# Visiting sixteen experts round by round over their four groups, and scaling their input rows by column chunks during the output projection

## The reference, cut to what matters

```python
h = rmsnorm(x, norm2_g[l]) * (1 + scale2) + shift2
x = x + gate2 * hier_moe(h, ...)

def hier_moe(h, w_rg, b_rg, w_re, b_re, w_gate, w_up, w_down):
    t = h.reshape(bsz * L, D)
    g_prob = softmax(t @ w_rg + b_rg)
    g_top, g_idx = lax.top_k(g_prob, 1)                      # one of 4 groups
    e_in = (the 4 expert logits of that group)
    e_top, e_idx = lax.top_k(softmax(e_in), TOP_K_INNER)     # two of its 4 experts
    e_id = g_idx * EXPERTS_PER_GROUP + e_idx
    hid = silu(t @ w_gate[e]) * (t @ w_up[e]) * gate[e]
    out = sum over e of hid @ w_down[e]
```

## Time and profile before

| | |
|---|---|
| median of 3 executions | 1426.71 us (1423.45 to 1427.87) |
| time of the profiled execution | 1427.36 us |
| its span, first to last instruction | 1425.3 us |
| granted TensorE clock, mean | 0.928 of full |
| TensorE matmul busy | 1195.7 us (84%) |
| DVE / ACT / POOL busy | 311.0 / 201.0 / 115.9 us |
| bytes moved | 401.09 MB |

### The profile page before, as it was taken

One profiled execution on the slowest core, in us unless ns is written; L12 is line 12 of the kernel. 1 busy time (PEld: TensorE's weight loads), 2 busy tenths in 40 slices (PEclk: granted clock), 3 DMA queues, 4 the chain that ended last, 5 costly groups with the idle time before them and its releaser, 6 DMA issues.

```text
span 1425.3 us, 16027 instructions
## 1 busy us (share of the span) xinstructions
PE 1195.7 (84%) x6320; PEld 643.4 (45%) x6321; DVE 311.0 (22%) x623; ACT 201.0 (14%) x385; POOL 115.9 (8%) x129
## 2 busy tenths in 40 slices
PE   2688999999999999999992299999988787787740
PEld 0235666665545455545542244444544444444420
DVE  0101221131122224120018510111111211111128
ACT  2002111012021222100012100110111111111102
POOL 2010000000000002000005100000000000000016
PEclk9778999989999999999996599999999999999975
DMA  9988787747657529652530468877999999999953
GB/s 332 421 339 274 286 343 277 278 163 280 251 206 284 220 71 360 229 188 79 221 118 33 177 252 302 311 278 293 384 407 413 411 414 400 390 412 412 426 205 114
DMA packets 71717, 401.09 MB, mean 281 GB/s; under 512 B 6489, under 2 KB 6713, under 8 KB 39645
## 3 DMA queue, kind: packets, MB, share of 16 engines
q1 hardware_dynamic: 63216, 368.59, 66.1%
q0 software_dynamic: 6944, 23.99, 5.1%
q10 hardware_dynamic: 1520, 7.98, 1.5%
HBM read 394.85 MB, written 17.22 MB: 289 GB/s over the span
## 4 chain that ended last, share of the span: by engine, by line
PE 65%; DMA 26%; DVE 6%; issue 1%; ACT 1%; POOL 0%; SPq 0%; POOLq 0%; DVEq 0%
PE bank L815 20%; DMA arena<-in_w_up_dram 20%; PE bank L892 10%; PE bank L1163 8%; PE bank L819 5%; PE bank L810 5%; DMA arena<-in_w_ada_dram 5%; PE bank L1160 5%; PE bank L1186 4%; PE bank L836 1%; PE bank L1183 1%; PE bank L910 1%; DVE arena L1480 1%; DVE arena L1481 1%; PE bank L1146 1%
## 5 line engine op out<-in xcount | busy, mean ns | idle before, releaser
L815 PE MATMUL bank<-arena 128*128 128x512 f32 x640 | 287.1, 599 | 0.0
L1160 PE MATMUL bank<-arena 128*64 128x256 f32 x1536 | 185.5, 399 | 60.6 <-DMA arena<-in_w_gate_dram 33.2
L815 PEld LDWEIGHTS bank<-arena 128*128 128x128 f32 x640 | 118.7, 191 | 136.5 <-issue 135.2
L1160 PEld LDWEIGHTS bank<-arena 128*64 128x64 f32 x1536 | 112.5, 143 | 138.3 <-DMA arena<-in_w_gate_dram 44.3
L892 PE MATMUL bank<-arena 128*128 128x320 f32 x512 | 142.3, 437 | 3.8 <-DVE arena L1258 3.8
L810 PE MATMUL bank<-arena 128*32 128x512 f32 x768 | 103.0, 679 | 44.2 <-DMA arena<-in_w_ada_dram 32.2
L892 PEld LDWEIGHTS bank<-arena 128*128 128x128 f32 x512 | 97.3, 191 | 50.7 <-issue 7.2
L1163 PE MATMUL bank<-arena 128*128 128x512 f32 x256 | 113.0, 602 | 6.9 <-issue 6.9
L1183 PE MATMUL bank<-arena 128*64 128x512 f32 x384 | 85.0, 595 | 6.0 <-DVE arena L1629 6.0
L1626 DVE SCALAR_TENSOR_TENSOR arena<-bank,arena 128x512 f32<-128x512 f32 x16 | 12.0, 751 | 347.7 <-PE bank L1160 232.7
L1163 PEld LDWEIGHTS bank<-arena 128*128 128x128 f32 x256 | 49.3, 193 | 69.4 <-issue 69.4
(11 more groups left out here) (314 smaller groups left out, 855.4 us busy)
## 6 DMA issues: line engine op xcount, KB each, us to landing
arena<-in_w_ada_dram SPq DMA_DIRECT2D x48, 2048.0 KB, 14.7
arena<-in_w_gate_dram SPq DMA_DIRECT2D x32, 2048.0 KB, 26.3
arena<-in_w_up_dram SPq DMA_DIRECT2D x32, 2048.0 KB, 27.1
arena<-in_w_down_dram SPq DMA_DIRECT2D x32, 2048.0 KB, 26.1
arena<-in_w_in_dram SPq DMA_DIRECT2D x20, 2048.0 KB, 7.8
arena<-in_w_out_dram SPq DMA_DIRECT2D x8, 2048.0 KB, 8.9
arena<-mod_final POOLq DMA_DIRECT2D x6, 1024.0 KB, 11.7
arena<-expert_rows SPq DMA_DIRECT2D x8, 512.0 KB, 7.8
```

Source lines behind the costliest of these rows:

```text
L815: return mm(bank[:, :], lhsT=xT_[:, t, OFF[j]:OFF[j] + P], rhs=w, start=start, stop=stop)
L1160: last = mm(PB[bank][64 * h:64 * h + 64, 0:HALF], lhsT=XeT[:, t0 + t, 0:64], rhs=slots_w[slot][:, t, HALF * h:HALF * h + HALF], start=star ...
```

## The change

Experts are visited as 0, 4, 8, 12, then 1, 5, 9, 13, and so on: SP loads weights in that order, and `by_visit` writes the columns of `top1` and `top2` so that column `i` of every table belongs to visit `i`. The scale of `h2p` is applied by column chunks in natural column order (`scaled(q)`), three DVE instructions behind each chunk of the output projection; factor and shift follow in one instruction per tile (`shifted(j)`) inside the routing. Tile 2 leaves ACT and POOL, no tile lies in W1 any more, all three stores are issued by ACT, `Xe` moves to another place and is cleared earlier, the transposes read every 16th column, and TensorE reads the number of passes before its first transposes.

```diff
-        h2p = [at(SA, D), at(MX + 2048, D), at(SLOT, D)]
+        h2p = [at(SA, D), at(HT + 4096, D), at(HT + 6144, D)]
...
@@ SP
-                    if isinstance(i, int) and s == W1:
-                        sp.wait_ge(h2_stored[2], 16)
...
-            expert(0, 0)
-            with sp.Fori(1, NE) as e:
-                expert(e, e)
+            for g in range(4):
+                expert(4 * g, g)
+            with sp.Fori(1, 4) as a:
+                for g in range(4):
+                    expert(a + 4 * g, 4 * a + g)
@@ POOL
             pool.wait_ge(x1_ready, 12)
-            pool.wait_ge(ssq2, 12)
-            pool.memset(arena[:, SA + 2048:MX], 0.0).then_inc(cleared, 1)
...
-            pool.tensor_tensor(o, o, by_t(a2b[0:DEC, 1, :]), ALU.mult).then_inc(h2_sample, 1)
...
-            pool.tensor_tensor(o, o, by_t(s2b[0:DEC, 1, :]), ALU.add).then_inc(h2_sample, 1)
...
-            pool.dma_start(h2_d[SEQ:TOK, :], h2p[2][0:DEC]).then_inc(h2_stored[2], 16)
-            pool.wait_ge(h2_ready, 2)
+            pool.memset(arena[:, SA + 2048:tables_end], 0.0).then_inc(cleared, 1)
+            pool.wait_ge(slot_used[W1], 16)
             pool.memset(Xe, 0.0).then_inc(cleared, 1)
@@ ACT
-            act.activation(by_t(h2p[2][0:DEC], out=True), by_t(x1[0:DEC, 2, :]), ACT.Copy, scale=st[0:DEC, 11:12]).then_inc(h2_sample, 1)
-            for j in range(2):
-                act.wait_ge(h2_ready, j + 1)
-                act.dma_start(h2_d[OFF[j]:OFF[j] + P, :], h2p[j]).then_inc(h2_stored[j], 16)
...
             act.activation(rt[:, :, 2:3], rt[:, :, 1:2], ACT.Exp).then_inc(gexp, 1)
+            for j in range(3):
+                act.wait_ge(h2_ready, j + 1)
+                act.dma_start(h2_d[OFF[j]:OFF[j] + NT[j], :], h2p[j][0:NT[j]]).then_inc(h2_stored[j], 16)
@@ TensorE
-                        last = tr(PB[2 + k][:, P * c:P * c + P], Xe[:, P * t:P * t + P], ident)
+                        last = tr(PB[2 + k][:, P * c:P * c + P], Xe[:, t::KT], ident)
...
             slot_info(0, 0)
+            pe.wait_ge(tables, 1)
+            passes = pe.value_load(nit[0:1, 0:1].bitcast(I32), min_val=1, max_val=PASSES)
             transpose_rows(0)
             slot_info(1, 1)
-            pe.wait_ge(tables, 1)
-            passes = pe.value_load(nit[0:1, 0:1].bitcast(I32), min_val=1, max_val=PASSES)
@@ DVE
+            def scaled(q):
+                if q == 0:
+                    dve.wait_ge(s2_in, 64)
+                cols = slice(N * q, N * q + N)
+                for j in range(3):
+                    n = NT[j]
+                    step(V.tensor_tensor(h2p[j][0:n, cols], x1[0:n, j, cols], a2b[0:n, STREAM[j], cols], ALU.mult))
...
+                if q < 3:
+                    scaled(q)
...
             V.tensor_scalar(col(3, 3), col(0, 3), 1.0 / D, EPS, ALU.mult, ALU.add).then_inc(var, 1)
+            scaled(3)
...
-            for j in range(2):
-                o = by_t(h2p[j], out=True)
-                step(V.scalar_tensor_tensor(o, by_t(x1[:, j, :]), col(9 + j), by_t(a2b[:, 0, :]), ALU.mult, ALU.mult))
-                V.tensor_tensor(o, o, by_t(s2b[:, 0, :]), ALU.add).then_inc(h2_ready, 1)
...
-            step(V.tensor_tensor(g4(top1), grid(goh, 3), grid(eoh1, 2), ALU.mult))
+            step(V.tensor_tensor(by_visit(top1), grid(goh, 3), grid(eoh1, 2), ALU.mult))
...
+            def shifted(j):
+                n = NT[j]
+                V.scalar_tensor_tensor(h2p[j][0:n], h2p[j][0:n], col(9 + j, 1, n), s2b[0:n, STREAM[j], :], ALU.mult, ALU.add).then_inc(h2_ready, 1)
+            shifted(0)
+            shifted(1)
...
             pick(0)
+            shifted(2)
             indices(0)
```

More of the change, by code:

```diff
@@ L183, in trunk @@
         yrow = at(0, 6, D)
-        Xe, XeT, Ye = at(HT, D), at(HT + 2048, KT, P), at(HT + 4096, D)
+        XeT, Xe, Ye = at(MX, KT, P), at(MX + 2048, D), at(HT + 4096, D)
         hid, hidT, sil = at(HT + 6144, N), at(HT + 6656, N), at(HT + 7168, N)
-        Pm, slotno = at(HT + 7680, 3, P), at(HT + 8064, P)
-        g2b, gfin = at(MX, 2, D), at(SA, D)
+        Pm, slotno = at(MX + 4096, 3, P), at(MX + 4480, P)
+        g2b, gfin = at(HT, 2, D), at(SA, D)
         ptr[0] = SA + 2048
@@ L201, in trunk @@
         hi, fold = take(1), take(P)
-        assert ptr[0] <= MX, ptr[0]
+        tables_end = ptr[0]
+        assert tables_end <= SA + 4096, ptr[0]
         PB = [ctx.enter_context(nc.psum_tensor(f"bank{i}", [P, N], F32)) for i in range(8)]
@@ L236, in trunk @@
             sem, ("modq_in", "modf_ready", "modf_stored", "g1_in", "s2_in", "xr_in"))
-        outp_read, x1_ready, ssq2, rstd2, h2_ready, h2_sample, cleared = map(
-            sem, ("outp_read", "x1_ready", "ssq2", "rstd2", "h2_ready", "h2_sample", "cleared"))
+        outp_read, x1_ready, ssq2, rstd2, h2_ready, cleared = map(
+            sem, ("outp_read", "x1_ready", "ssq2", "rstd2", "h2_ready", "cleared"))
         h2_stored = [sem(f"h2_stored{j}") for j in range(3)]
@@ L364, in expert @@
                 for s, kind, half in order:
-                    if not isinstance(i, int) or before_moe[s]:
+                    if not isinstance(i, int) or i + before_moe[s]:
                         sp.wait_ge(slot_used[s], i + before_moe[s])
-                    if isinstance(i, int) and s == W1:
-                        sp.wait_ge(h2_stored[2], 16)
                     if kind == "d":
@@ L384, in _ @@
                 with sp.Fori(1, passes) as p:
-                    with sp.Fori(0, NE) as e:
-                        expert(e, NE * p + e)
+                    with sp.Fori(0, 4) as a:
+                        for g in range(4):
+                            expert(a + 4 * g, NE * p + 4 * a + g)
             sp.wait_ge(routed, 1)
@@ L483, in _ @@
             pool.wait_ge(x1_ready, 12)
-            pool.wait_ge(ssq2, 12)
-            pool.memset(arena[:, SA + 2048:MX], 0.0).then_inc(cleared, 1)
-            pool.wait_ge(s2_in, 64)
-            pool.wait_ge(h2_sample, 1)
-            o = by_t(h2p[2][0:DEC], out=True)
-            pool.tensor_tensor(o, o, by_t(a2b[0:DEC, 1, :]), ALU.mult).then_inc(h2_sample, 1)
-            pool.wait_ge(h2_sample, 2)
-            pool.tensor_tensor(o, o, by_t(s2b[0:DEC, 1, :]), ALU.add).then_inc(h2_sample, 1)
-            pool.wait_ge(h2_sample, 3)
-            pool.dma_start(h2_d[SEQ:TOK, :], h2p[2][0:DEC]).then_inc(h2_stored[2], 16)
-            pool.wait_ge(h2_ready, 2)
+            pool.memset(arena[:, SA + 2048:tables_end], 0.0).then_inc(cleared, 1)
+            pool.wait_ge(slot_used[W1], 16)
             pool.memset(Xe, 0.0).then_inc(cleared, 1)
@@ L754, in _ @@
             act.activation(st[:, 6:9], st[:, 3:6], ACT.Sqrt).then_inc(std, 1)
-            act.wait_ge(slot_used[W1], 16)
-            act.wait_ge(rstd2, 1)
-            act.activation(by_t(h2p[2][0:DEC], out=True), by_t(x1[0:DEC, 2, :]), ACT.Copy, scale=st[0:DEC, 11:12]).then_inc(h2_sample, 1)
-            for j in range(2):
-                act.wait_ge(h2_ready, j + 1)
-                act.dma_start(h2_d[OFF[j]:OFF[j] + P, :], h2p[j]).then_inc(h2_stored[j], 16)
             act.wait_ge(gexp_in, 1)
@@ L1472, in _ @@
             V.tensor_scalar(col(3, 3), col(0, 3), 1.0 / D, EPS, ALU.mult, ALU.add).then_inc(var, 1)
+            scaled(3)
             dve.wait_ge(std, 2)
             V.reciprocal(col(9, 3), col(6, 3)).then_inc(rstd2, 1)
-            dve.wait_ge(rstd2, 1)
-            dve.wait_ge(s2_in, 64)
-            for j in range(2):
-                o = by_t(h2p[j], out=True)
-                step(V.scalar_tensor_tensor(o, by_t(x1[:, j, :]), col(9 + j), by_t(a2b[:, 0, :]), ALU.mult, ALU.mult))
-                V.tensor_tensor(o, o, by_t(s2b[:, 0, :]), ALU.add).then_inc(h2_ready, 1)
             dve.wait_ge(cleared, 1)
@@ L1488, in _ @@
             V.tensor_scalar(fold, iota, 63.5, -64.0, ALU.is_gt, ALU.mult)
-            step(V.memset(rk, -1.0))
+            V.memset(rk, -1.0)
             for k in range(3):
@@ L1495, in _ @@
             step(V.tensor_reduce(lg[0:DEC, 2, :].unsqueeze(2), by_chunk[0:DEC, 2], AX.X, ALU.add))
+            dve.wait_ge(rstd2, 1)
             for j in range(3):
@@ L1529, in _, with by_visit @@
             V.tensor_tensor(rt[:, :, 1:2], rt[:, :, 5:6], rt[:, :, 4:5], ALU.subtract).then_inc(gexp_in, 1)
-            step(V.tensor_tensor(g4(top1), grid(goh, 3), grid(eoh1, 2), ALU.mult))
-            step(V.tensor_tensor(g4(top2), grid(goh, 3), grid(eoh2, 2), ALU.mult))
+            def by_visit(a):
+                return a.rearrange("p j (e g) -> p j g e", g=4)
+            step(V.tensor_tensor(by_visit(top1), grid(goh, 3), grid(eoh1, 2), ALU.mult))
+            step(V.tensor_tensor(by_visit(top2), grid(goh, 3), grid(eoh2, 2), ALU.mult))
             step(V.memset(top1[DEC:P, 2, :], 0.0))
@@ L1593, in _ @@
             slot_tables(slice(0, NE))
-            dve.wait_ge(h2_sample, 3)
             pick(0)
+            shifted(2)
             indices(0)
```

## The result

The changed kernel takes 1378.39 us (median of 4 executions, 1376.91 to 1379.37) against 1426.82 us before: a ratio of 0.9666, 95% interval 0.9653 to 0.9678, faster by 48 us. The forecast was 1380 us. The profiled execution took 1379.37 us, its span is 1377.6 us.

The account below looks back on a forecast made before the run. The expert loop was bound first by TensorE in four long visits, then by weight loads. From 1427.36 us, 31.0 for the loop and 16.0 for the front gave 1380.4, so 1380 us for a median; range 1366 to 1395 us.

Parts of the forecast that it names:

- the loop: Expert loop: new visit order gains 35.8 us, extra gathered and scattered rows cost 4.8 us, so 31.0 us less.
- the front: From output projection to expert loop: six steps sum to -16.0 us, first expert matmul at 805.0 instead of 820.98 us.
- does a long visit let the loads run dry?: Long visits in the loop: loads have 9.9 us to spare and short visits win back the delay, so costed at nothing.
- The routing starts earlier: Ahead of the loop: routing starts at 762.2 us instead of 785.45, -23.2 us.
- the sum by that rule: Front's sum if Xe's memset does not slow `scaled(3)`: -16.0 us; by the rows alone it would be -14.1.
- The routing without a memset beside it: First small routing instructions: the memset of `Xe` no longer lies beside them, -0.8 us (0 to 1.86).
- `shifted(0)` and `shifted(1)`: Routing, behind the mask: two DVE instructions, 4.7 us together, partly in former DVE idle time, +2.9 us.
- `shifted(2)` and its store: Before the gather: 2.4 us instruction and 4.1 us store delay the gather's issue, +4.7 us.
- The register read: TensorE's 6.93 us idle before its first expert matmul: moving one read ahead of the gather's landing gives -1.5 us (0 to -3.5).
- the stride: Transposes of gathered rows reading every 16th column take longer in the first two visits: +1.9 us (0 to 2.6).
- the slower rival: Expert loop: TensorE's clock falls to 1.2 GHz for long visits after idle short ones, 1468 us; chance 0.03.
- The signs: Wrong if DMA share under 0.95 from 870 to 1300 us, clock well below 0.9 in long visits, or gather past 795 us.

Follow-up runs that it names:

- the read back: Changed kernel with TensorE's read of the number of passes back behind the first transposes: 1378.65 us.
- the loads later: Changed kernel with three 1 MB loads for the kernel's end issued only after TensorE has done with the first weight slot: 1375.52 us.

## Why the prediction was right, step by step

The time was in the range, 1.6 us from the forecast for a median, and both large terms were right in mechanism and nearly in size: the loop gave 28.4 us where I had 31.0, the front 17.8 where I had 16.0. That the total came nearer than its terms is luck: the two errors have opposite signs, and the 1.6 us from ahead of the front, in no sum of mine, are spread between executions.

- **The loop.** The last down load for the second visit was issued 47.9 us after the first matmul, as said (47.4). From there to the last up landing it took 460.2 us where I had 453.3 + 4.8 = 458.1, and the 508.1 us of the whole loop lie above the 501 to 506 that I had named as a sign. The step that was off is "does a long visit let the loads run dry?", which I had costed at nothing. DMA was not full near the end of the later long visits (busy columns as before, then clock, DMA share, GB/s):

```profile
970.00:980.00 10.00, 10.00 (x29) 4.31 (x29) 0.46 (x1) 0.46 (x1) 0.00 (x0) 1.00 0.88 333
...
1100.00:1110.00 10.00, 10.00 (x27) 4.34 (x27) 0.35 (x1) 0.35 (x1) 0.00 (x0) 1.00 0.86 329
...
1230.00:1240.00 10.00, 10.00 (x24) 4.39 (x24) 0.18 (x2) 0.00 (x0) 0.94 (x1) 1.00 0.82 278
```

  The missing shares of these and the 10 us behind each (0.96, 0.93, 0.86) make 7 us over three long visits. My 9.9 us to spare counted the 16 DMA engines as one, and took nothing for the time from issue to landing. The trace's records of landings speak against both. A load raises its semaphore in 16 steps, and from 870 us on the first step of a load comes 4 to 14 us before the last. Near the end of each of the three visits the first part of the second up load had landed (969.68, 1100.30 and 1232.51 us) 3.0, 2.5 and 3.5 us before SP issued the next load (972.67, 1102.78 and 1236.02 us), and the first part of that one landed 7 us after its issue. Anywhere else from the second visit on the next load was issued no more than 0.1 us after such a first landing, mostly many us before it. So the loads did run dry, for the engines that were ahead. An estimate from the packets' own times, against 83/65 of those in the 65 loads before: gathers and scatters took 3.0 us more of all 16 engines, where I had 4.8 for the extra rows, engines without work 6.4 us, where I had nothing, and the loads 2.6 us less; together that is about the excess of 6.9 us over the bare 453.3. (My 29.8 rows for a short visit should be 30.2, the 640 - 278 rows of the other groups over twelve visits, which leaves the 1.6 us as they are.)
- **The routing starts earlier**: 24.1 us against 23.2. `scaled(3)` began at 756.94, during the memset of `Xe`, and its three instructions were over 1.5 us after L1472, where I had 2.1. POOL did hold L1472 (1.24 us for three numbers) until that memset ended at 758.08 us. Three tensor_tensor instructions over as many numbers, at 756.41 to 756.66 us in the same memset, took 0.15 to 0.16 us each; the first of `scaled(3)` took 1.17 us and ended with L1472, and whether it waited for L1472 or for the memset no row tells. This is what the Trainium skill, SBUF — State Buffer, Who interferes with whom, says of tensor_scalar, and of tensor_tensor beside work of GpSimd that only writes; the trace agrees for those four, and the sum by that rule was the nearer one.
- **The routing without a memset beside it**: 1.1 us shorter, against 0.8.
- **`shifted(0)` and `shifted(1)`**: 4.61 us for two, and 2.8 us on the path against 2.9. **`shifted(2)` and its store**: 4.7 us on the path, as forecast; the gather is issued 8.58 us behind `pick(0)`.
- **The register read** (-1.5) and **the stride** (+1.9) were both wrong and cancelled. The runs with the read back, the loads later and the stride undone show no price for either that can be told. What I had put down to reads and loop entries is the time to reach the code of the long visit's branch. The number that I had chosen for the stride came from transposes that fed evacuations, and their time was not that of the stride; what it was, no run shows.
- **The rivals.** The clock was 0.97 to 1.00 from 850 us on, taken by stretches of 50 to 100 us. Inside them the slower rival had a grain of truth: behind a wait of some 3 us, two of the three later long visits began with TensorE at 1.2 GHz for a part (0.66 in the 4 us from 932 us, 0.57 from 1196, but 1.00 from 1064) and took 46.8 and 46.7 us, against 45.1 for the third and far from the rival's 76. The order was worth its price without the rest of the change, and the last store landed after 4.24 us, where I had 4.1.
- **The signs.** None of those for being wrong came: from 870 to 1300 us DMA stood at 0.99 and the clock at 0.98, and the gather went out at 784.37 us.

## What to carry to other kernels

Where a loop has visits of two lengths and loads that can run only a fixed number of buffers ahead, the sum over visits is not the time: count for each place whether the longer ones stand one behind the other, and put them where short ones can use up the lead. Such a sum, from two durations and one load rate in the trace, came within 3 us in 536. What it left out is that the 16 DMA engines do not keep step: time to spare has to be counted for the one that is furthest ahead, and from issue to landing. A term that is small and taken from "what lies in this idle time" should be tested before it is believed: here two were wrong, and the idle time had another cause, worth 8 to 9 us to a swap of two branches.

## What the runs showed of the hardware

- TensorE's idle time ahead of the first expert matmul was 6.9 to 7.7 us when the branch led to the code that stands second, 4.7 to 4.8 us when three 1 MB loads were moved out of that time, and 1.1 us when it led to the code that stands next, be the visit short or long. Where it was long, a 16 KB packet of the kind `instruction` ended 1.6 to 1.9 us before that matmul, and the loads delayed its start by 3 us.
- A tensor_scalar over three numbers took 1.24 us and ended with POOL's memset; three tensor_tensor instructions of the same size, in the same memset, took 0.15 to 0.16 us. In the kernel before, three more tensor_scalar instructions (L1491) took 1.4 to 1.6 us each beside the memset of `Xe`; their counterparts in the changed kernel (L1483), with no memset beside them, took 0.10 to 0.16 us.
- Transposes that read every 16th column take 196 ns instead of 141 to load, and no more time on the whole: 3.62 us for 16 of them, against 3.58.
- The first and the last of the 16 parts of a 2 MB load landed 4 to 14 us apart from 870 us on, where DMA was full; where a load was issued after the first part of the one before had landed, its own first part came 7 us after the issue.
